# Clearing a stage's semaphores with four engines, a quarter each, instead of with VectorE alone

## What is computed

```python
def first_block(x, c, ctx, ...):
    ...
    h_lat = modulate(rms_norm(x, norm_mix_g[layer]), sh1, sc1)
    y_lat, y_ctx = token_mixer(h_lat, h_ctx, need_ctx, w_in[layer], conv_w[layer], ...)
    x = x + g1 * y_lat
    h = modulate(rms_norm(x, norm_ffn_g[layer]), sh2, sc2).reshape(-1, D_MODEL)
    x = x + g2 * moe_ffn(h, *moe_w).reshape(x.shape)
    return rms_norm(x, final_norm_g)

def second_block(x, meta, rel_bias, ...):
    for l in range(DEPTH_2):
        ...
        h = h + jnp.concatenate([a_out, b_out, c_out], axis=-1) @ w_out[l]
        u = rmsnorm(h, norm_ff[l])
        h = h + jnp.square(jax.nn.relu(u @ w_ff1[l])) @ w_ff2[l]
    return rmsnorm(h, final_norm)[:, N_META:]
```

## The kernel before

| stage | semaphores | times run |
|---|---|---|
| preamble: constants, transposes | 5 | 1 |
| modulation, first norm | 13 + 4 held | 1 |
| gates and biases | 11 | 1 |
| delta rule (cleared by `clear_all`, L170 to L176, see below) | 69 | 1 |
| linear attention: projection | 3 | 1 |
| in a loop over 4 heads (L1215): l1, l2, l3, l4, l5 | 3 + 1 held, 4, 5, 5, 1 | 4 each |
| its end | 1 + 1 held | 1 |
| merge: four projections by `split_project` | 13 each | 4 |
| merge: gates (between them) | 2 | 1 |
| norm (`rsqrt_stage`) | 5 | 1 |
| router | 6 | 1 |
| experts | 31 with those held | 1 |
| transposition of the sum | 3 | 1 |
| experts' overflow (a loop that has nothing to do on these inputs) | 31 | 1 |
| residual, final norm of the first block | 6 | 1 |
| second block, both layers, to the output | 77 with those held | 1 |

## Time and profile before

### The profile page before, as it was taken

The page is one execution under the profiler, slowest core; times in us unless marked ns, Lnnn a source line. Parts: engine busy times, 40 slices in busy tenths (PEclk is TensorE's granted clock), DMA queues, the critical chain, the costliest instruction groups (busy, mean ns, idle before and its releaser), DMA issues. The chain is left out here.

```text
span 3425.0 us, 45252 instructions
## 1 busy us (share of the span) xinstructions
PE 3105.7 (91%) x17512; PEld 2571.5 (75%) x17513; DVE 2142.9 (63%) x3249; ACT 1608.2 (47%) x2191; POOL 143.7 (4%) x175
## 2 busy tenths in 40 slices
PE   7989999978887669999999999999698799997998
PEld 2568887945567557888887888888586699985997
DVE  2135565534434449989889889899566466574664
ACT  0034444411112327777777777777343245442453
POOL 0032322200000000000000000000000000000000
PEclk9899999987777868999999999999897599995998
DMA  7451100011213258999999999999162055540453
GB/s 258 139 89 32 44 26 1 1 40 38 60 44 104 99 200 298 361 340 350 358 339 356 348 343 358 341 353 358 65 205 71 10 165 175 149 139 1 129 183 108
DMA packets 255955, 605.59 MB, mean 177 GB/s; under 512 B 25378, under 2 KB 86025, under 8 KB 255625
## 3 DMA queue, kind: packets, MB, share of 16 engines
q1 hardware_dynamic: 254668, 602.39, 50.8%
q10 hardware_dynamic: 1085, 0.45, 0.0%
HBM read 598.39 MB, written 4.39 MB: 176 GB/s over the span
## 5 line engine op out<-in xcount | busy, mean ns | idle before, releaser
L1713 DVE TENSOR_TENSOR moe_raw_r<-moe_raw,moe_hi 128x2048 fp32r<-128x2048 f32 x320 | 720.2, 2284 | 14.8 <-ACT moe_hi L1651 14.8
L1651 ACT ACTIVATE moe_hi<-moe_raw 128x2048 fp32r<-128x2048 f32 x320 | 599.9, 1907 | 103.1 <-PE banks L1575 102.7
L2432 PE MATMUL banks<-xs_r,w_hi 128*128 128x272 f32 (+1 forms) x1632 | 475.4, 291 | 28.5 <-DVE w_raw_r L2856 17.6
L2436 PE MATMUL banks<-xs_r,w_raw_r 128*128 128x272 f32 (+1 forms) x1632 | 472.0, 289 | 0.0
L2433 PE MATMUL banks<-xs_r,w_hi 128*128 128x272 f32 (+1 forms) x1632 | 469.8, 288 | 0.0
L2677 ACT ACTIVATE w_hi<-w_raw 128x512 fp32r<-128x512 f32 (+1 forms) x416 | 256.7, 619 | 252.4 <-PE banks L2436 212.2
L1575 PE MATMUL banks<-moe_raw_r,moe_xs 128*128 128x512 f32 x1024 | 346.3, 421 | 0.0
L2432 PEld LDWEIGHTS banks<-xs_r,w_hi 128*128 128x128 f32 x1632 | 310.7, 190 | 34.5 <-issue 23.4
L2856 DVE TENSOR_TENSOR w_raw_r<-w_raw,w_hi 128x512 fp32r<-128x512 f32 (+1 forms) x416 | 272.8, 676 | 81.4 <-ACT w_hi L2677 77.5
L2436 PEld LDWEIGHTS banks<-xs_r,w_raw_r 128*128 128x128 f32 x1632 | 310.8, 190 | 2.7
L2433 PEld LDWEIGHTS banks<-xs_r,w_hi 128*128 128x128 f32 x1632 | 311.2, 191 | 0.2
(11 more groups left out here) (477 smaller groups left out, 5376.0 us busy)
## 6 DMA issues: line engine op xcount, KB each, us to landing
moe_raw<-in_w_gu SPq DMA_DIRECT2D x256, 1024.0 KB, 9.4
moe_raw<-in_w_down SPq DMA_DIRECT2D x128, 1024.0 KB, 10.6
w_raw<-in_w_ff SPq DMA_DIRECT2D x256, 256.0 KB, 3.0
w_raw<-in_w_in SPq DMA_DIRECT2D x112, 256.0 KB, 2.7
ring_mod<-in_w_mod SPq DMA_DIRECT2D x12, 2048.0 KB, 8.3
wq<-in_w_in SPq DMA_DIRECT2D x32, 512.0 KB, 4.7
wh<-in_w_in SPq DMA_DIRECT2D x10, 1024.0 KB, 8.5
mrg_raw<-in_w_in SPq DMA_DIRECT2D x16, 512.0 KB, 3.8
```

The lines of the kernel that those rows point to most:

```text
L1651: act.activation(hi[n % HI_SLOTS][:, :], raw[n % UNITS][:, :], ACT.Copy).then_inc(his, 1)
L1713: dve.tensor_tensor(rest[n % UNITS][:, :], raw[n % UNITS][:, :], hi[n % HI_SLOTS][:, :].bitcast(F32), ALU.subtract).then_inc(los, 1)
L2432: pe.matmul(bank, w_hi, x[:, 0, 0:n_cols], start=first, stop=False)
L2436: ins = pe.matmul(bank, w_lo, x[:, 0, 0:n_cols], start=False, stop=last)
```

## The change

The semaphores of a stage and those held are put in one list, and the second block of `stage` now gives each of four engines every fourth of them: VectorE from the first on, ScalarE from the second, TensorE from the third, SyncE from the fourth. `clear_all` stays as it is. The lines below move by 17.

```diff
         with nc.Block(no_gpsimd_drain=True) as block:
+            every = [*sems, *held]
+
             @block.vector
             def _(dve):
-                for s in (*sems, *held):
+                for s in every[0::4]:
                     dve.sem_clear(s)
+
+            @block.scalar
+            def _(act):
+                for s in every[1::4]:
+                    act.sem_clear(s)
+
+            @block.tensor
+            def _(pe):
+                for s in every[2::4]:
+                    pe.sem_clear(s)
+
+            @block.sync
+            def _(sp):
+                for s in every[3::4]:
+                    sp.sem_clear(s)
```

## The result

The changed kernel takes 3403.2 us (median of five runs, 3402.1 to 3406.2) against 3421.6 us (now five runs, 3421.3 to 3426.6), a ratio of 0.9944 with a 95% interval from 0.993 to 0.9959, which is 14 to 24 us. So it is 18 us faster, 0.56%; 16 us were forecast. One execution of before_again, which took 12084 us where its ten others took 3420 to 3427 us, is left out of all that follows.

A forecast was written before the change was run, and what follows sets the result against it. DVE's 327 semaphore clears, 27.5 us, were taken to bound the crossings between stages; less 0.5 us (DVE) and 10.8 us (PE) remaining, the gain was 16.2 us, so 3422.24 − 16.2 = 3406 us, range 3401 to 3415 us.

The forecast's parts named there:

- DVE's clears bound every crossing, and nothing hides them: All 37 stage crossings: DVE reports last, its 327 clears cost 27.5 us, and no running transfer swallows a gain.
- The sum for the crossings: Over 37 crossings: 27.5 us of DVE clears less 0.5 and 10.8 us remaining, so 16.2 us less.
- PE's clear: Each of PE's 76 clears in the crossings: taken at 120 ns, between 83 and 202 ns.
- the value that adds PE's 30 ns to DVE's price: PE's clear costs the same 30 ns more than DVE's as its meeting event does: 113 ns.
- the scaled one: Rival: PE's clear scales with its meeting event to 202 ns, gain only 10.0 us, 3412 us; chance 0.10.
- PE's fixed part: PE's later start in the 31 crossings where it sets the length: 55 ns each, 1.7 us together.
- the hole of 0.4 us at 1055.9: A gap on DVE where two clears start 0.5 us apart instead of 0.08; cited under late code.
- The crossings of one semaphore stay: Crossings with a single semaphore: DVE keeps the one clear, so nothing changes there.
- The queue at the semaphores: Rival: clears of four engines go one at a time; gain 9.8 us (3412 us) or none (3422 us); chance 0.07.
- Late code: Rival: new clear blocks on three more engines are fetched late, holes of 0.4 us per crossing, 3436 us; chance 0.03.
- Crossings are all: Stages between crossings: nothing of the computation is moved, so the time falls by the crossings' 16.2 us.
- a way to lose the gain by chance: Rival: stages give the gain back through PE's granted clock, only the last crossing's gain left, 3418 us; chance 0.06.

The follow-up runs named there:

- before_again: The kernel before, unchanged, run again for a second profile: 3423.5 us beside 3422.5 us for before, ratio 1.0.
- end_five: The kernel before, with each of the last stage's 77 semaphores cleared five times by DVE: 3448.8 us against 3423.1 us.
- rest_thrice: The kernel before, with all stages except the linear attention's and the last clearing each semaphore three times on DVE: 3451.3 us against 3421.9 us.
- balanced: The kernel before, with clears dealt to four engines by each one's measured offset and price: 3392.2 us against 3423.1 us.
- mid_twice: The kernel before, with all stages except the last clearing each semaphore twice on DVE: 3453.5 us against 3423.1 us.
- ranges: The kernel before, with VectorE alone clearing each run of neighbouring semaphores by one instruction in the stages: 3391.8 us against 3422.5 us.

## Why the prediction was right, and where its terms were off

*DVE's clears bound every crossing, and nothing hides them.* Right. end_five and rest_thrice put 25.7 and 28.2 us of clears into the crossings and found 25.7 and 29.5 us in the time. The medians of the change, 18.4 and 17.6 us, hold the 15.4 us of the crossings in full.

*The sum for the crossings.* 16.2 us forecast, 15.4 us measured. Term by term: the last crossing 4.4 and 4.43 us; the two of 31 3.1 and 2.96; the four of 13 2.7 and 2.58; the ten of five 2.4 and 2.05; the rest 3.6 and 3.4 us. PE's clear, taken at 120 ns, is 117 ns: near the value that adds PE's 30 ns to DVE's price, and far from the 202 ns of the scaled one. The term that was mis-sized is PE's fixed part, taken as 55 ns behind DVE's. A crossing in which PE clears lasts 0.444 + 0.117 × its clears, one in which DVE is last 0.355 + 0.083 × its clears, so the difference is 89 ns: PE reports 55 ns later, as taken, and POOL's release follows PE's report 34 ns later than DVE's (166 and 132 ns between their starts). Over 31 crossings that is 1.05 us. Of the hole of 0.4 us at 1055.9, which I did not count, nothing was left in the changed kernel: 0.4 us the other way. Small holes in the changed kernel, among them 0.15 us in the crossing of 17, and PE's 117 instead of 120 ns make up the rest.

*The crossings of one semaphore stay.* Right, 0.44 us in both.

*The queue at the semaphores.* Ruled out, by DVE's unchanged 83 ns and by balanced.

*Late code.* In the changed kernel no crossing of a stage is more than 0.15 us longer than its price says; the one larger hole, SP's in the last crossing, lies in the shadow of PE's clears. In the other kernels a few holes of 0.2 to 0.4 us showed, some of them between two clears that stand in a row. What makes a hole stays open: in the trace of before the DMA queues move no instructions in the 3 us ahead of either hole, the one at 1055.9 or the one at 3421.7, nor during them. The prediction had the two agree with the rule of the Trainium skill on fetches (Runtime: NRT & Kernel Launch, "Instruction fetch mechanics"), a taken branch that waits for its page; the trace does not bear that out.

*Crossings are all.* For this change that stands within the noise: the medians moved 2 to 3 us farther than the crossings, and the interval can't tell that from nothing. For edits beside it, it is wrong (mid_twice, ranges, balanced), and I held the clock only for a way to lose the gain by chance. The forecast of 3406 us lies 2.8 us above 3403.2 us: the crossings' gain was put 0.8 us too high, the median of before had moved from 3422.24 to 3421.62 us, and 3.0 us beyond the crossings were missing. That the first runs against the others is luck.

## What to carry to other kernels

Where all engines meet, what counts is the latest of them: before a serial piece is dealt out, take each engine's price for it, and its offset at the meeting; an equal share for the dearest engine cost 1.4 us more in the crossings than leaving it out (32.2 against 30.8 us). Before dealing out many small instructions, look whether one can do them all: one engine with ranges (3392 us) does as well as four with the best split (3392 us), and 3388 us with the delta rule's included. And a gap between stages can cost more than its length where PE's clock changes in the stages around it, as mid_twice shows (22.4 us of gaps, about 30 us of time); compare medians and their intervals with the sum of the gaps, not one profile with another.

## What I had not expected of the hardware

- A clear's step is 117 ns on PE, 83 ns on DVE, 66 ns on ACT and 55 to 61 ns on SP, for DVE and PE whether one engine clears or four; ACT and SP were never measured alone.
- A range clear is recorded at 79 ns for five semaphores and 415 ns for the longer of two runs that hold 69 together: 5 to 6 ns for each further semaphore (from one, 55 ns, to five; from five to at most 68).
- Four engines together cleared 77 semaphores in 1.4 us.
- POOL's release follows 34 ns later when PE's report is the last.
- 4.4 us less in crossings of the linear attention brought 9.4 us (5.8 to 12.7), and 22.4 us more over all crossings but the last cost 30.5 us (25.3 to 34.9), while 29.2 us more outside the linear attention cost 29.5 us (22.6 to 30.8).
- The same stage with the same 92 matmuls took 26.6 us at a granted clock of 0.63 and 29.6 us at 0.54, in one execution.
